# Old values issued behind their keys, and the sample states stored in two large pieces from ScalarE's queue

## Chip, cores and metric

The kernel runs on one core of a Trainium2 chip. The metric is the device time of one execution in microseconds, the median of several runs. Five engines run side by side and meet at semaphores: TensorE (PE), VectorE (DVE), ScalarE (ACT), GpSimd (POOL) and SyncE (SP). SyncE computes nothing here; its queue issues nearly all transfers.

## What is computed

One inference step of a two-layer decoder trunk in float32, for a prompt of 256 tokens and for 8 sampled sequences of 8 new tokens each. A layer is, cut to what matters:

```
h = RMSNorm(x); p = h @ w_in, split among three token mixers
A: dilated sliding-window attention, 8 heads of 64; the sampled tokens read a cache of 2048 old keys and values
B: RWKV-7 recurrence, 8 heads, state S (64 x 64 per head), which is also an output (new_wkv_*)
C: window attention, 16 query heads on 2 kv heads, old window of 128
x = x + concat(A, B, C) @ w_out
x = x + SwiGLU(RMSNorm(x))
```

The new keys, values, shift rows and states of both layers are outputs too.

## The kernel before

The weights stream through two raw buffers; ScalarE and VectorE split each block in a high and a low part, and TensorE multiplies with both. Between the projections `w_in` and `w_out` of a layer stand `rwkv(l)` and `attention(l)`, written out by hand in each engine's program. The change is in the queue around these two.

**Attention of the sampled tokens.** The 8 sequences are taken in pairs, q = 0 to 3. For a pair the old keys lie in `cK[0]` and `cK[1]`, the old values in `cV[0]` and `cV[1]`, each in three quads (4, 4 and 2 key tiles). For a pair:

- SyncE loads them with `cache(b, which, quad)` (L463 to L482): two loads of 512 KB for quads 0 and 1, one for quad 2, and a small one of 64 KB for the window cache (`ckc`, `cvc`). A sequence's keys are five large loads and one small, 2.6 MB, and its values the same.
- VectorE turns each quad of keys in place as it lands (`turn`, L1374), four transposes of the full size and two of half the size to a pair, waiting for each quad's own semaphore.
- TensorE computes the scores in `keys(q)`, with pieces of the prompt's attention placed between: `prompt_scores(a)`, and near its end `turned_probs(carry)`, which needs what ScalarE's `scale(carry)` wrote. Its last score product posts `sc`. Then come `probabilities(q)` and `values(q)`, which posts `pvq` once for each quad of values it is done with.
- ScalarE runs, for each pair, `exp(carry)`, `scale(carry)`, `exp(a)`, `turned_probs(carry)`, `scale(a)` and so on, and `exps(q)` for the samples. Here carry and a are the prompt's head pairs; for q = 0 they are 2 and 3. Ahead of `exps(0)` it waits for `snk`, which counts one small load and three stores of new keys.

The last pair (q = 3) has its values in `cK[0]` and in `cX`, the latter lying where the states are held until they are stored.

**SyncE's order in attention.** Keys of sequences 1 and 0; the small load `snk` (L492); a wait for `kvc`, which ScalarE posts when all nine blocks of new rows lie in `tk` (L837); three stores of new keys (L496, L497); values of sequences 0 and 1; seven stores of new values and window rows. Then for q = 1, 2, 3 `next_keys(q)`, which waits for `sc`, and `next_values(q)`, which waits for `pvq` quad by quad. Between the keys and the values of q = 1 stands `states_out()`. Before the load into `cX` at q = 2 SyncE waits until the states have left. Behind the last pair come the loads of `w_out`.

**The states.** ScalarE copies the states from PSUM to `Sout` (128 partitions: two head halves of 64; sequence, head, column) and `SoutP` for the prompt, and posts `Soc` (L849). This is done before attention starts. `states_out()` (L509 to L515) stores them with one transfer for each sequence and head half, 16 of 64 KB, and two for the prompt.

Of the kernel before, what the change touches and what calls it, by code (L numbers as in the profile page):

```python
# [39 lines left out]
DEPTH = 2  # L40
SEQ = 256
NB = 8
# [4 lines left out]
HD = 64  # L47
# [127 lines left out]
def build(nc, I, O, at):  # L175
    ctx = ExitStack()
    with ctx:
# [7 lines left out]
        def place(name, shape, offset, dt=F32):  # L185
            return nc.alloc_sbuf_tensor_at(name, shape, dt, offset=offset)
# [66 lines left out]
        Sout = place("Sout", [P, NB, 4, HD], RX + 10240)  # L253
        SoutP = place("SoutP", [P, 4, HD], RX)
# [44 lines left out]
        sem = {n: ctx.enter_context(nc.semaphore("s_" + n)) for n in names}  # L299
# [64 lines left out]
        def _(sp):  # L364
# [76 lines left out]
            for l in range(DEPTH):  # L441
# [21 lines left out]
                def cache(b, which, quad):  # L463

                    last = which == "V" and b // 2 == LASTQ
                    s = sem[f"cK{quad}{b % 2}" if last or which == "K" else f"cV{quad}"]
                    dst, small = (cK, ckc) if which == "K" or last else (cV, cvc)
                    ahead = last and b % 2 == 1
                    if ahead:
                        s = sem["cX"]  # L470
                    rows = I["cache_a_" + which.lower()][l, b].rearrange("r h d -> r (h d)")
                    old = rows[0:1536].rearrange("(j g r) c -> j g r c", j=3, r=16)
                    new = rows[1536:2048].rearrange("(p r) c -> p r c", p=P)
                    for j in range(2 * quad, min(2 * quad + 2, 5)):
                        to = (cX if ahead else dst[b % 2])[:, 2 * j:2 * j + 2, :]
                        if j < 3:
                            src = old[j, :, 0:8, :].rearrange("g (r i) c -> g r (i c)", i=2)
                            sp.dma_start(to.rearrange("p i c -> p (i c)"), src).then_inc(s, 16)  # L478
                        else:
                            sp.dma_start(to, new[:, 2 * j - 6:2 * j - 4, :]).then_inc(s, 16)  # L480
                    if quad == (2 if which == "K" or last else 1) and not ahead:
                        sp.dma_start(small[b % 2][:], I["cache_c_" + which.lower()][l, b].rearrange("r h d -> r (h d)")).then_inc(s, 16)  # L482
# [6 lines left out]
                cache(1, "K", 2)  # L489
                for quad in range(3):  # L490
                    cache(0, "K", quad)
                sp.dma_start(snk[:], I["c_sink"][l].rearrange("k g -> (k g)").unsqueeze(1).unsqueeze(2).broadcast_to([16, TS, 1])).then_inc(sem["snk"], 16)  # L492
                sp.wait_ge(sem["kvc"], 9 * (l + 1))
                for q in range(2):
                    rows = slice(q * P, (q + 1) * P)
                    sp.dma_start(O["new_a_k_prompt"][l, 0, rows].rearrange("t h d -> t (h d)"), tk[0][:, q, :]).then_inc(sem["snk"], 16)  # L496
                sp.dma_start(O["new_a_k_sample"][l].rearrange("b t h d -> (b t) (h d)"), tk[0][0:NS, 2, :]).then_inc(sem["snk"], 16)  # L497
                for quad in range(3):
                    cache(0, "V", quad)
                    cache(1, "V", quad)  # L500
                for q in range(2):
                    rows = slice(q * P, (q + 1) * P)
                    sp.dma_start(O["new_a_v_prompt"][l, 0, rows].rearrange("t h d -> t (h d)"), tk[1][:, q, :]).then_inc(sem["out"], 16)
# [1 line left out]
                sp.dma_start(O["new_c_v_prompt"][l, 0].rearrange("t h d -> t (h d)"), tk[2][:, 1, P:2 * P]).then_inc(sem["out"], 16)  # L505
                for name, src in (("new_a_v_sample", tk[1][0:NS, 2, :]), ("new_c_k_sample", tk[2][0:NS, 2, 0:P]), ("new_c_v_sample", tk[2][0:NS, 2, P:2 * P])):
                    sp.dma_start(O[name][l].rearrange("b t h d -> (b t) (h d)"), src).then_inc(sem["out"], 16)

                def states_out():  # L509
                    for h2 in range(2):  # L510
                        for b in range(NB):
                            sp.dma_start(O["new_wkv_sample"][l, b].rearrange("(f h) i j -> h i f j", h=2)[h2],  # L512
                                         Sout[h2 * HD:(h2 + 1) * HD, b]).then_inc(sem["souts"], 16)
                        sp.dma_start(O["new_wkv_prompt"][l, 0].rearrange("(f h) i j -> h i f j", h=2)[h2],
                                     SoutP[h2 * HD:(h2 + 1) * HD]).then_inc(sem["souts"], 16)  # L515

                def next_keys(q):
                    sp.wait_ge(sem["sc"], 4 * l + q)
                    for b2 in range(2):
                        for quad in range(3):  # L520
                            cache(2 * q + b2, "K", quad)

                def next_values(q):
                    if q == LASTQ:
                        sp.wait_ge(sem["sc"], 4 * l + q + 1)
                    for quad in range(3):
                        if q < LASTQ:
                            sp.wait_ge(sem["pvq"], 3 * (4 * l + q - 1) + quad + 1)
                        cache(2 * q, "V", quad)
                        if q < LASTQ:  # L530
                            cache(2 * q + 1, "V", quad)
                        elif quad == 2:
                            sp.dma_start(ckc[1][:], I["cache_c_v"][l, NB - 1].rearrange("r h d -> r (h d)")).then_inc(sem["cK21"], 16)
                for q in range(1, NB // 2):
                    next_keys(q)
                    if q == 1:
                        states_out()
                    if q == 2:
                        sp.wait_ge(sem["souts"], 16 * 18 * (l + 1))
                        for quad in range(3):  # L540
                            cache(NB - 1, "V", quad)
                    next_values(q)
# [16 lines left out]
            sp.wait_ge(sem["ends"], 80)  # L559
            sp.wait_ge(sem["out"], 16 * 9 * DEPTH)  # L560
            sp.wait_ge(sem["snk"], 64 * DEPTH)
            sp.wait_ge(sem["souts"], 16 * 18 * DEPTH)


        @block.gpsimd
# [62 lines left out]
        def _(act):  # L628
            want = Tally()

            def take(name, by=1):
                act.wait_ge(sem[name], want(sem[name], by))
# [151 lines left out]
            for l in range(DEPTH):  # L784
# [79 lines left out]
                def window_keys():  # L864
                    take("ktp")
                    act.activation(kcT[:].rearrange("p b k -> p (b k)"), PS[:, 7, 0:2 * P], ACT.Copy).then_inc(sem["ktc"], 1)
# [74 lines left out]
                turned_probs(1)  # L941
                output(1)
                window_keys()
                for q in range(NB // 2):
                    carry, a, b, c = partners(q)
                    exp(carry)
                    scale(carry)
                    exp(a)
                    turned_probs(carry)
                    scale(a)  # L950
                    output(carry)
                    turned_probs(a)
                    if q == 0:
                        act.wait_ge(sem["snk"], 64 * (l + 1))
                    exps(q)
                    output(a)
                    turned_sample(q)
                    if q < LASTQ:
                        query_rows(q + 1)
                        if b:  # L960
                            exp(b)
                            scale(b)
                            turned_probs(b)
                        window_keys()
                        if b:
                            output(b)
# [1178 lines left out]
```

## Time and profile before

| | |
|---|---|
| median of 3 runs | 3316.92 us (3314.89 to 3319.36) |
| the profiled execution's own time | 3315.85 us |
| its span, from the first instruction to the last | 3314.0 us |
| mean granted TensorE clock | 0.973 of full speed |
| TensorE busy | 3167.2 us, 96% |
| moved by DMA | 501.29 MB, 151 GB/s over the span |

Times in rows are microseconds from the span's start. A line such as L1374 is a line of the kernel. Where a row ends in brackets, the number in them is the idle time ahead of it and the arrow says what ended it. A DMA share of 1.00 means that all 16 DMA engines of the core were busy; values a little above 1 come from how packets are timed.

### The profile page before, as it was taken

The numbers are of one execution on the slowest core, as the hardware profiler recorded it, in microseconds if no ns is written. First come the engines' busy times: TensorE is split into PE (matmuls) and PEld (weight loads), VectorE is DVE, ScalarE is ACT, GpSimd is POOL, SyncE is SP. The second block draws the span as 40 slices with busy tenths as digits, with TensorE's granted clock in tenths as the row PEclk, the third lists the DMA queues.
The fourth block names the chain that finished last, engine by engine and source line by source line (L and its number), as shares of the span: only waits on it lengthen the run. The fifth ranks groups of instructions, "written<-read, shape, count | busy, mean of one in ns | idle before, by whom it ended". The sixth has DMA issues, their size and how long they took to land.

```text
span 3314.0 us, 62786 instructions
## 1 busy us (share of the span) xinstructions
PE 3167.2 (96%) x26351; PEld 3014.4 (91%) x26351; DVE 1756.7 (53%) x2112; ACT 1148.8 (35%) x1537; POOL 74.6 (2%) x157
## 2 busy tenths in 40 slices
PE   8999878899999999999999988789999999999998
PEld 7999755799999999999999987459999999999998
DVE  5555567455554454454545664765555545545544
ACT  3332264442332232322434313644323322323234
POOL 1000010000000000000000000100000000000000
PEclk9999888999999999999999998989999999999999
DMA  7553049765554554555565610787655545555454
GB/s 212 162 132 68 2 182 341 176 144 152 152 152 138 154 152 139 161 146 141 156 185 139 140 27 3 256 311 171 152 145 147 152 137 162 142 152 155 136 148 128
DMA packets 849061, 501.29 MB, mean 151 GB/s; under 512 B 96640, under 2 KB 823184, under 8 KB 848464
## 3 DMA queue, kind: packets, MB, share of 16 engines
q1 hardware_dynamic: 848492, 499.02, 53.7%
q8 instruction: 115, 1.88, 0.2%
q14 instruction: 34, 0.28, 0.0%
q10 hardware_dynamic: 420, 0.10, 0.0%
HBM read 485.71 MB, written 13.37 MB: 151 GB/s over the span
## 4 chain that ended last, share of the span: by engine, by line
PE 87%; DVE 4%; SPq 4%; DMA 3%; ACT 2%; issue 1%; POOL 0%; ACTq 0%; DVEq 0%
PE PS L1520 85%; DMA cK<-in_cache_a_k 2%; SPq L478 1%; PE PS L1521 1%; SPq L512 1%; DMA raw<-in_w_out 1%; SPq L480 1%; DVE cK L1374 0%; DVE wl L1010 0%; ACT wh L639 0%; SPq L482 0%; DVE S0T L1324 0%; DVE rt L1128 0%; ACT psm L876 0%; POOL S0in L588 0%
## 5 line engine op out<-in xcount | busy, mean ns | idle before, releaser
L639 ACT ACTIVATE wh<-raw 128x2048 fp32r<-128x2048 f32 (+1 forms) x408 | 711.7, 1744 | 1241.7 <-PE PS L1520 1211.1
L1010 DVE TENSOR_TENSOR wl<-raw,wh 128x2048 fp32r<-128x2048 f32 (+1 forms) x408 | 848.6, 2080 | 409.9 <-ACT wh L639 409.2
L1520 PE MATMUL PS<-fh,wh 128*128 128x320 f32 x2816 | 870.6, 309 | 0.0
L1520 PE MATMUL PS<-fh,wl 128*128 128x320 f32 x2816 | 870.1, 309 | 0.0
L1520 PE MATMUL PS<-fl,wh 128*128 128x320 f32 x2816 | 870.1, 309 | 0.0
L1520 PEld LDWEIGHTS PS<-fl,wh 128*128 128x128 f32 x2816 | 528.5, 188 | 0.2
L1520 PEld LDWEIGHTS PS<-fh,wh 128*128 128x128 f32 x2816 | 528.5, 188 | 0.2
L1520 PEld LDWEIGHTS PS<-fh,wl 128*128 128x128 f32 x2816 | 528.5, 188 | 0.0
L1520 PE MATMUL PS<-hh,wh 128*128 128x320 f32 (+2 forms) x1696 | 521.4, 314 | 1.6 <-DVE wl L1010 1.6
L1520 PE MATMUL PS<-hh,wl 128*128 128x320 f32 (+2 forms) x1696 | 513.3, 308 | 0.0
L1520 PE MATMUL PS<-hl,wh 128*128 128x320 f32 x1664 | 510.2, 310 | 0.0
L1520 PE MATMUL PS<-ah,wh 128*128 128x320 f32 x1408 | 435.7, 309 | 0.2 <-DVE wl L1010 0.2
L1520 PE MATMUL PS<-ah,wl 128*128 128x320 f32 x1408 | 435.1, 309 | 0.0
L1520 PE MATMUL PS<-al,wh 128*128 128x320 f32 x1408 | 435.0, 309 | 0.0
L1520 PEld LDWEIGHTS PS<-hh,wh 128*128 128x128 f32 x1696 | 318.0, 191 | 5.3 <-issue 1.9
L1520 PEld LDWEIGHTS PS<-hh,wl 128*128 128x128 f32 x1696 | 315.2, 189 | 0.0
L1520 PEld LDWEIGHTS PS<-hl,wh 128*128 128x128 f32 x1664 | 312.0, 188 | 1.4
L1520 PEld LDWEIGHTS PS<-ah,wh 128*128 128x128 f32 x1408 | 264.3, 188 | 0.8 <-issue 0.5
L1520 PEld LDWEIGHTS PS<-al,wh 128*128 128x128 f32 x1408 | 264.3, 188 | 0.0
L1520 PEld LDWEIGHTS PS<-ah,wl 128*128 128x128 f32 x1408 | 264.3, 188 | 0.0
L668 ACT ACTIVATE ge<-gt 128x320 f32<-128x320 f32 x88 | 41.5, 472 | 488.2 <-DVE gt L1050 488.2
L1050 DVE TENSOR_TENSOR gt<-PS,rsb 128x320 f32<-128x320 f32 x88 | 43.3, 492 | 226.1 <-PE PS L1520 226.1
(329 smaller groups left out, 2513.0 us busy)
## 6 DMA issues: line engine op xcount, KB each, us to landing
raw<-in_w_gate SPq DMA_DIRECT2D x88, 1024.0 KB, 5.6
raw<-in_w_up SPq DMA_DIRECT2D x88, 1024.0 KB, 5.6
raw<-in_w_down SPq DMA_DIRECT2D x128, 704.0 KB, 4.8
raw<-in_w_in SPq DMA_DIRECT2D x56, 1024.0 KB, 5.6
cK<-in_cache_a_k SPq DMA_DIRECT2D x80, 512.0 KB, 9.0
cV<-in_cache_a_v SPq DMA_DIRECT2D x60, 512.0 KB, 9.1
raw<-in_w_in SPq DMA_DIRECT2D x32, 512.0 KB, 5.6
raw<-in_w_out SPq DMA_DIRECT2D x32, 512.0 KB, 4.7
```

Source lines behind the costliest of these rows:

```text
L478: sp.dma_start(to.rearrange("p i c -> p (i c)"), src).then_inc(s, 16)
L480: sp.dma_start(to, new[:, 2 * j - 6:2 * j - 4, :]).then_inc(s, 16)
L512: sp.dma_start(O["new_wkv_sample"][l, b].rearrange("(f h) i j -> h i f j", h=2)[h2], Sout[h2 * HD:(h2 + 1) * HD, b]).then_inc(sem["souts"] ...
L639: act.activation(wh[j][:, 0:kts], raw[j][:, 0:kts], ACT.Copy).then_inc(sem["wh"], 1)
L668: act.activation(ge[:], gt[:], ACT.Tanh, scale=0.5).then_inc(sem["gexp"], 1)
L1010: tt(wl[j][:, 0:kts], raw[j][:, 0:kts], wh[j][:, 0:kts].bitcast(F32), ALU.subtract).then_inc(sem["wl"], 1)
L1050: tt(gt[:], PS[:, 0, 0:TOK], rsb[:], ALU.mult).then_inc(sem["ev"], 1)
L1520: mm = lambda out, lhsT, rhs, start=True, stop=True: pe.matmul(out, lhsT, rhs, start=start, stop=stop, skip_group_check=True)
L1521: tr = lambda out, x: pe.transpose(out, x, con[0:x.shape[0], at["ident"][0]:at["ident"][0] + x.shape[0]])
```

## The change

First, the values of sequences 0 and 1 are issued right behind the keys, ahead of the load `snk`, the wait for `kvc` and the stores of new keys. Second, `states_out()` is gone from SyncE. ScalarE issues the states' stores ahead of its loop over the pairs: for each head half one store with the states of all eight sequences (512 KB, 64 partitions of 8 KB in the buffer, 32 runs of 256 B for each partition in memory) and one for the prompt. The counts that wait for these stores go from 18 to 4 a layer.

```diff
                 for quad in range(3):
                     cache(0, "K", quad)
+                for quad in range(3):
+                    cache(0, "V", quad)
+                    cache(1, "V", quad)
                 sp.dma_start(snk[:], ...)
                 sp.wait_ge(sem["kvc"], 9 * (l + 1))
                 ...
-                for quad in range(3):
-                    cache(0, "V", quad)
-                    cache(1, "V", quad)
                 ...
-                def states_out():
-                    for h2 in range(2):
-                        for b in range(NB):
-                            sp.dma_start(O["new_wkv_sample"][l, b].rearrange("(f h) i j -> h i f j", h=2)[h2],
-                                         Sout[h2 * HD:(h2 + 1) * HD, b]).then_inc(sem["souts"], 16)
-                        sp.dma_start(O["new_wkv_prompt"][l, 0].rearrange("(f h) i j -> h i f j", h=2)[h2],
-                                     SoutP[h2 * HD:(h2 + 1) * HD]).then_inc(sem["souts"], 16)
                 ...
                 for q in range(1, NB // 2):
                     next_keys(q)
-                    if q == 1:
-                        states_out()
                     if q == 2:
-                        sp.wait_ge(sem["souts"], 16 * 18 * (l + 1))
+                        sp.wait_ge(sem["souts"], 16 * 4 * (l + 1))
...
                 output(1)
                 window_keys()
+                act.wait_ge(sem["Soc"], 9 * (l + 1))
+                for h2 in range(2):
+                    rows_h = slice(h2 * HD, (h2 + 1) * HD)
+                    act.dma_start(O["new_wkv_sample"][l].rearrange("b h i j -> (b h) i j").rearrange("(r h) i j -> h i r j", h=2)[h2],
+                                  Sout[rows_h].rearrange("p b f j -> p (b f) j")).then_inc(sem["souts"], 16)
+                    act.dma_start(O["new_wkv_prompt"][l, 0].rearrange("(f h) i j -> h i f j", h=2)[h2], SoutP[rows_h]).then_inc(sem["souts"], 16)
                 for q in range(NB // 2):
                     carry, a, b, c = partners(q)
                     exp(carry)
```

The query columns of `w_in` are loaded, far from the change, by two transfers for a block, each of 128 partitions by 16 runs of 256 B (L379); the prediction comes back to them.

## Rows read from the trace of the kernel before

**Rows 1.** The page's part 1: busy us (share of the span) xinstructions.

```profile
PE 3167.2 (96%) x26351; PEld 3014.4 (91%) x26351; DVE 1756.7 (53%) x2112; ACT 1148.8 (35%) x1537; POOL 74.6 (2%) x157
```

**Rows 2.** Chain that ended last, 450 to 615 us: shares, then start, us, what.

```profile
by line: PE PS L1520 22.6%; DMA cK<-in_cache_a_k 15.2%; SPq L478 11.6%; SPq L512 8.9%; DMA raw<-in_w_out 6.0%; issue 4.5%; SPq L480 4.5%; DVE cK L1374 4.2%; PE PS L1521 3.0%; SPq L482 2.5%; ACT psm L876 2.2%; ACT tk L837 1.9%; SPq L386 1.6%
...
527.15 14.34 DMA cK<-in_cache_a_k
```

**Rows 3.** SyncE's queue in order of time, layer 0: start, us, issues.

```profile
459.73 0.57 SPq L492 DMA_DIRECT2D snk<-in_c_sink  x1
471.04 0.82 SPq L496 DMA_DIRECT2D out_new_a_k_prompt<-tk  x2
...
472.52 3.24 SPq L478 DMA_DIRECT2D cV<-in_cache_a_v  x5
...
487.29 2.99 SPq L478 DMA_DIRECT2D cK<-in_cache_a_k  x3
...
495.45 10.09 SPq L512 DMA_DIRECT2D out_new_wkv_sample<-Sout  x8
...
512.17 3.54 SPq L478 DMA_DIRECT2D cV<-in_cache_a_v  x5
...
519.61 1.88 SPq L478 DMA_DIRECT2D cK<-in_cache_a_k  x3
```

**Rows 4.** Windows of 4.25 us: each engine's busy time, clock, DMA share, GB/s.

```profile
465.50:469.75 4.25, 3.61 (x21) 2.43 (x22) 4.21 (x4) 2.36 (x6) 0.00 (x0) 0.63 0.35 125
...
508.00:512.25 4.25, 3.35 (x84) 2.06 (x98) 3.04 (x7) 1.07 (x5) 0.00 (x0) 0.50 0.47 97
...
529.25:533.50 4.25, 4.25 (x72) 3.35 (x74) 3.39 (x4) 2.70 (x10) 0.00 (x0) 0.74 1.03 411
```

**Rows 5.** Waits over the whole span: us in total, times, longest.

```profile
DVE cK L1374 <- DMA cK<-in_cache_a_k: 13.2, 24, 3.2
```

**Rows 6.** VectorE in order of time: first turn of a pair's keys.

```profile
532.07 2.31 DVE L1374 STREAM_TRANSPOSE cK<-cK 128x2048 f32<-128x2048 f32 x1 [0.83 <-DMA cK<-in_cache_a_k]
...
565.25 2.31 DVE L1374 STREAM_TRANSPOSE cK<-cK 128x2048 f32<-128x2048 f32 x1 [1.34 <-DMA cK<-in_cache_a_k]
...
2127.05 2.31 DVE L1374 STREAM_TRANSPOSE cK<-cK 128x2048 f32<-128x2048 f32 x1 [2.03 <-DMA cK<-in_cache_a_k]
...
2166.22 2.31 DVE L1374 STREAM_TRANSPOSE cK<-cK 128x2048 f32<-128x2048 f32 x1 [3.25 <-DMA cK<-in_cache_a_k]
...
2199.20 2.31 DVE L1374 STREAM_TRANSPOSE cK<-cK 128x2048 f32<-128x2048 f32 x1 [0.54 <-DMA cK<-in_cache_a_k]
```

**Rows 7.** SyncE's queue, layer 1: the third pair's keys.

```profile
2155.04 1.83 SPq L478 DMA_DIRECT2D cK<-in_cache_a_k  x3
```

**Rows 8.** ScalarE in order of time, layer 0 and layer 1.

```profile
476.35 1.49 ACT L888 ACTIVATE psm<-psm,sums 128x128 f32<-128x128 f32 x4 [0.31 <-DVE sums L1365]
...
2107.97 1.49 ACT L888 ACTIVATE psm<-psm,sums 128x128 f32<-128x128 f32 x4 [0.31 <-DVE sums L1365]
2113.18 0.40 ACT L876 ACTIVATE psm<-psm,nm 128x128 f32<-128x128 f32 x1 [3.72 <-DVE nm L1358]
...
2121.03 1.41 ACT L903 ACTIVATE smA<-smA,snm 128x1344 f32<-128x1344 f32 x1
```

**Rows 9.** TensorE in order of time inside keys(0), both layers.

```profile
483.25 1.09 PE L1520 MATMUL PS<-cK,qd 32*32 32x320 f32 x31 [2.19 <-issue]
484.27 1.54 PE L1521 MATMUL PS<-con,psm 128*128 128x128 f32 x6
...
2113.35 0.55 PE L1521 MATMUL PS<-con,psm 128*128 128x128 f32 x3
2115.80 0.49 PE L1521 MATMUL PS<-con,psm 128*128 128x128 f32 x3 [1.90 <-issue]
```

**Rows 10.** State stores' issue durations (ns min/median/max); two loads of 2048 runs.

```profile
L512 SPq DMA_DIRECT2D out_new_wkv_sample<-Sout x32: 616/638/2389, 495.4 to 2144.1; - x32
...
207.65 2.02 SPq L379 DMA_DIRECT2D raw<-in_w_in  x2
```

More of the change, by code:

```diff
@@ L561, in _ @@
             sp.wait_ge(sem["snk"], 64 * DEPTH)
-            sp.wait_ge(sem["souts"], 16 * 18 * DEPTH)
+            sp.wait_ge(sem["souts"], 16 * 4 * DEPTH)
         @block.gpsimd
```

## Prediction

> **What bounds the kernel now.** I read the page's table of busy times first. TensorE is busy 96% of a span of 3314.0 us [rows 1], so over most of the kernel no transfer can buy anything. That is an average over stages, so next comes the chain of work that ended last, asked only for the stretch of layer 0's attention that the change touches, 450 to 615 us. There TensorE's busiest line holds 22.6%, a transfer of old keys 15.2%, and lines of SyncE's queue 11.6% (L478, cache loads), 8.9% (L512, the state stores) and more [rows 2]. This stage is set by loads and by the queue that issues them.
>
> The queue's timeline shows how [rows 3]. SyncE has issued the first pair's keys by 459.73. It then stands at the wait for `kvc` until 471.04 and issues the first pair's values only at 472.52. Keys(1), the second pair's, go out at 487.29, when TensorE has finished with the first. Then come 18 state stores, from 495.45 until 512.17, and only behind them the second pair's values, 512.17 to 519.57, and the third pair's keys, from 519.61.
>
> The table by windows shows what this leaves of the DMA engines [rows 4]. They are empty two thirds of the time at 465.5 to 469.75 (share 0.35), when SyncE waits, and half the time at 508.00 to 512.25 (share 0.47, 97 GB/s), when only state stores are there. Where big loads are queued they run full, 411 GB/s. I use 405 GB/s. A pair's keys, ten loads of 512 KB and two small ones, are 5.2 MB and take 12.9 us; its values take as long.
>
> Who waits for the keys is VectorE, whose transposes (L1374) feed the scores. Its 24 waits for them sum to 13.2 us [rows 5]. It turns a pair's keys in about 11.9 us when nothing is late: four transposes of 2.31 us [rows 6], two of half the size, and small operations between. The instruction before each turn is its own, so each such wait lies on the loop that sets the stage: keys landed, turned, scores, `sc`, next keys issued. Gaps at the first turn of a pair are 0.83 and 1.34 us in layer 0, and 2.03, 3.25 and 0.54 us in layer 1 [rows 6].
>
> **The change, part by part.**
>
> *Values(0) and (1) ahead of the wait.* These are 15 cache loads and the two small ones inside them, all on SyncE. They are moved ahead of one sink load and three key stores; nothing is added. Issue starts at 459.73. The keys' remaining transfer comes first in the same queue, so I take it as undisturbed. Keys are done by about 466.7 and values by 466.7 + 12.9 = 479.6 instead of about 487. The stores of new rows (1.47 MB, 3.7 us) follow, to 483.3. The wait for `kvc` is then reached near its end, perhaps 2 us late, and the rest is issued before 487.29. ScalarE waits for the sink load and the three key stores only ahead of `exps(0)`, where its next work starts at 2121.03 in layer 1 [rows 8]; they should land by about 2114 to 2120. Cost nothing; if that cover fails, about 1 us.
>
> *State stores off SyncE.* 18 issues vanish, 16.7 us of its time (495.45 to 512.17), a median of 0.64 us each with stalls on top [rows 10]. SyncE can then issue the second pair's values behind `pvq`, whose quads TensorE releases before 504, in place of 512.17. The next keys go at `sc`.
>
> What is late next? For each later pair I ask whether its keys can land before VectorE wants them; VectorE's new start is that of its row, less the gap and less what was gained before (532.07 - 0.83 - 0.8 = 530.4; 565.25 - 1.34 - 2.6 = 561.3). Layer 0: keys(1) from 487.3 land by 502, and VectorE starts at 495.1 and needs its last quad at about 505. Values(1) are through by 515. Keys(2) go at about 518.6 and land by 533; VectorE starts at 530.4 and needs the last at 541. Then come the odd last value load and values(2), to about 552. Keys(3) go at 554.7 and land by 569; VectorE is ready at 561.3 and needs the last at 572. Layer 1 is tighter for keys(1), since the stores on ScalarE's queue still run at 2117. They land by 2136, with about 1 us to spare. Keys(2) there were issued at 2155.04 by a late SyncE [rows 7] and can now go at 2148.4, since keys(1) start 2.6 us sooner. So VectorE bounds each loop and its key waits go. The sum is 24 waits, 13.2 us, less 1.0 us kept for pieces that will not close: **-12.2 us**. No other work hides it: the loop runs from each turn through the scores to the next pair's keys, on to `w_out`, and the stage after it waits for all.
>
> *Four issues on ScalarE.* They stand in front of exp(2), so exp(2), scale(2), exp(3), and behind them TensorE's turned_probs(2) in the middle of keys(0), queue up behind them. The added wait for `Soc` is for ScalarE's own earlier copies, done long before. The slack is read off the timelines. In layer 0 scale(2) ends at 476.35 + 1.49 = 477.84, and TensorE takes its result at 484.27 [rows 8, 9]: 6.4 us. In layer 1 it ends at 2109.46 and exp(3) starts at 2113.18, after 3.72 us idle; TensorE turns at 2113.35, slack 3.9 us, with a hole of 1.90 us of its own before 2115.80.
>
> The price of an issue is not shown for this shape on this queue. From below: four issues at the 0.62 us of SyncE's state stores [rows 10] are 2.5 us, and cost nothing. The nearest row by pieces is the query columns of `w_in`. There two loads of 128 x 16 runs of 256 B, the same 2048 runs as one new store, were issued back to back in 2.02 us [rows 10]. With two small ones at 0.62 that makes 3.3 us, inside both slacks. From above: the last issue may have to wait until the first store and its small one have drained. Drained beside loads: 97 GB/s at share 0.47 is 206 GB/s of full engines, so a layer's 1.18 MB of states is 5.7 us of engine time and half of it 2.9 us. If SyncE's backlog (474.3 to 483.3, 9.0 us) goes through alongside, the stall is 11.9 us, costing 11.9 - 6.4 = 5.5 us in layer 0 and 11.9 - 3.9 = 8.0 us in layer 1, **0 to +13.5 us**. I take 0, by the nearest row.
>
> Full engines are seen here behind one queue only [rows 4]. A rule of the Trainium skill speaks against the change at this point. The Trainium skill, "DMA: Bandwidth & Descriptors", section "Queues, rings and completion order", says that each DMA engine alternates between the queue rows that have work, a packet at a time. By it the 256 B runs and the 4 KB runs of the values take turns, so the stores drain slowly while the backlog lasts, and the sum would lean to the upper end, near 0 instead of -12.2; that is the mechanism of rivals A and B. No row here has two busy queues, so the trace neither agrees nor disagrees.
>
> **Sum.** The profiled execution took 3315.85 us, 1.07 below the median of the three runs, 3316.92. 3315.85 - 12.2 = 3303.7; against the median 3304.7. I say **3305 us**.
>
> **The rivals.**
>
> *A: ScalarE stalls part of the way (chance 0.22).* Two queues share the engines and the second store is held 5 to 11 us. For it: SyncE's own state-store issues stretch to 2.39 us at the worst, behind queued loads [rows 10]. Against it: the 2.02 us pair. Cost 0 to 11.7 us over both layers, say 5: about 3310, between 3306 and 3316.
>
> *B: ScalarE stands until both stores are gone (0.07), the one that ends slower.* The place is the issue of the last store. If it is held until all of SyncE's backlog and all 5.7 us of states are through, that is 14.7 us from 474.3 to 489: 8.3 us over the slack in layer 0 and 10.8 in layer 1, 19.1 against a gain of 12.2, so about 3324. It decides above a hold of 11.3 us per layer, where (11.3 - 6.4) + (11.3 - 3.9) = 12.3 eats the gain. Against it: it takes a queue that accepts nothing while 2048 runs are pending, and [rows 10] had a second such load accepted within 2 us of the first.
>
> *C: the waits go but the time only moves (0.16).* The bytes are the same, and later pairs are loaded at the full rate either way (411 GB/s at 529 to 533 [rows 4]). If keys(2) and (3) stay at the engines' pace behind values, or TensorE's holes of 2 us "for nothing that the profile shows" (2.19 us inside keys(0) [rows 9]) fall in other places, only 4 to 8 us are gained: 3308 to 3313. For it: the third pair's last keys took 14.34 us to land [rows 2]. Against it: that was behind values issued late, and the idle stretches of [rows 4] are what the change fills.
>
> *Forecast (0.55):* all key waits gone and ScalarE inside its slack, own range 3299 to 3309; its low end is the whole 13.2 us and 4 us for TensorE, which ran at a granted clock of 0.50 after such a wait [rows 4].
>
> **Numbers.** Within 0.2% is about what a measurement of this kernel can tell from no change: 6.6 us, so faster means below 3310.3. Faster: 0.54 of the forecast, 0.09 of A, 0.07 of C, 0.70. Slower: B and its edge, 0.08. Same: 0.22. The range runs from the forecast's low end to the far end of A, 3299 to 3316.
>
> **What would show it.** Right: values(0) issued from 460; nothing idle at 465 to 470 but the engines full; keys(1) landed before each turn; VectorE's key waits near 1 us in total instead of 13.2; third pair's keys at 518 to 519; four issues on ScalarE taking under 4 us in each layer. Wrong: an issue on ScalarE longer than 3 us with exp(2) behind it, keys(0) ending later than 488 in layer 0, or transposes that still wait for keys.

## The result and the profile after

The changed kernel takes 3323.63 us, the median of 12 runs (3320.81 to 3328.14). The kernel before, measured again beside it, takes 3318.21 (12 runs, 3313.59 to 3322.15). The ratio is 1.002, 95% interval 1.0011 to 1.0029: slower by 0.2%, 5.4 us by the two medians and some 6.6 us by the ratio, where 12 us of gain were forecast. The time lies above the range. It is the one that rival B named, 3324. The profiled execution took 3323.82 us with a span of 3322.0 us, 8.0 us longer than before.

The page's part 1 after, beside [rows 1]:

```profile
PE 3160.4 (95%) x26351; PEld 3011.2 (91%) x26351; DVE 1755.5 (53%) x2112; ACT 1148.5 (35%) x1537; POOL 74.6 (2%) x157
```

No engine has more to do; the time is waiting. The waits over the whole span (us in total, times, longest) say whose:

```profile
ACT psm L866 <- issue: 27.5, 2, 14.5
...
DVE cK L1370 <- DMA cK<-in_cache_a_k: 2.3, 6, 0.6
```

The lower line is the one forecast. VectorE's waits for the keys are down from 13.2 us in 24 waits [rows 5] to 2.3 us in 6. The upper line is new. Before exp(2), ScalarE stands "for issue", twice and 27.5 us in all, that is once in each layer. What it does in that time is on its own timeline, layer 0 first and then layer 1 (start, us, what; ACTq is ScalarE's queue of issues):

```profile
474.81 0.72 ACTq L937 DMA_DIRECT2D out_new_wkv_sample<-Sout  x1
475.56 7.50 ACTq L939 DMA_DIRECT2D out_new_wkv_prompt<-SoutP  x1
483.09 2.30 ACTq L937 DMA_DIRECT2D out_new_wkv_sample<-Sout  x1
485.42 4.24 ACTq L939 DMA_DIRECT2D out_new_wkv_prompt<-SoutP  x1
489.71 0.40 ACT L866 ACTIVATE psm<-psm,nm 128x128 f32<-128x128 f32 x1 [14.53 <-issue]
...
2114.09 7.35 ACTq L939 DMA_DIRECT2D out_new_wkv_prompt<-SoutP  x1
...
2126.77 0.40 ACT L866 ACTIVATE psm<-psm,nm 128x128 f32<-128x128 f32 x1 [12.98 <-issue]
```

The first large store is accepted in 0.72 us. The small one behind it takes 7.50 us to issue, the second large one 2.30 and its small one 4.24. The four take 14.8 us (474.81 to 489.66) where 3.3 was assumed. TensorE's timeline shows what queues behind them, the turned_probs(2) of [rows 9]:

```profile
493.43 1.54 PE L1517 MATMUL PS<-con,psm 128*128 128x128 f32 x6 [9.28 <-ACT psm L878]
```

It began at 484.27 before; now TensorE idles 9.28 us for ScalarE's scale(2). The table by windows (length, each engine's busy time, granted clock, DMA share, GB/s) shows both sides of the change, beside [rows 4]:

```profile
465.50:469.75 4.25, 2.69 (x17) 1.65 (x18) 4.21 (x5) 3.28 (x9) 0.00 (x0) 0.74 1.02 392
482.50:486.75 4.25, 0.83 (x31) 0.24 (x31) 0.00 (x0) 0.00 (x0) 0.00 (x0) 0.75 1.08 343
486.75:491.00 4.25, 0.00 (x0) 0.00 (x0) 0.00 (x0) 1.29 (x7) 0.00 (x0) 0.50 0.85 188
495.25:499.50 4.25, 4.25 (x48) 2.55 (x16) 2.45 (x7) 2.61 (x8) 1.22 (x8) 0.50 0.35 88
499.50:503.75 4.25, 2.78 (x14) 1.88 (x14) 2.36 (x4) 2.36 (x3) 0.71 (x5) 0.50 0.99 364
503.75:508.00 4.25, 4.25 (x24) 3.23 (x22) 2.06 (x4) 2.45 (x10) 0.00 (x0) 0.50 1.02 406
508.00:512.25 4.25, 4.25 (x83) 2.67 (x84) 4.25 (x2) 3.31 (x19) 0.00 (x0) 0.94 0.98 388
```

At 465.5 to 469.75 the DMA engines are full (1.02, 392 GB/s; the share was 0.35 before), as intended. From 482.5 to 491 three compute engines do next to nothing. After this idle time the granted clock is 0.50, the 1.2 GHz level, up to 508, though TensorE is busy again (4.25 of 4.25 us in two of these windows); it works through the rest of keys(0) and the work behind it at half the clock. Low windows are nothing new in themselves: before, the clock was 0.50 at 508.00 to 512.25 [rows 4].

SyncE's queue shows where the time goes on, beside [rows 3] and [rows 7]:

```profile
460.84 3.12 SPq L478 DMA_DIRECT2D cV<-in_cache_a_v  x5
...
496.45 1.90 SPq L478 DMA_DIRECT2D cK<-in_cache_a_k  x3
...
533.25 1.83 SPq L478 DMA_DIRECT2D cK<-in_cache_a_k  x3
...
2133.50 1.89 SPq L478 DMA_DIRECT2D cK<-in_cache_a_k  x3
...
2166.85 2.50 SPq L478 DMA_DIRECT2D cK<-in_cache_a_k  x3
```

Keys(1) of layer 0 leave at 496.45 instead of 487.29, 9.2 us late, of which 0.9 were there on entry to the stage. The third pair's leave at 533.25 instead of 519.61, 13.6 us late: this loop takes 36.8 us (496.45 to 533.25) where it took 32.3 before, so it loses instead of gaining. The clock is down for its first 11.5 us; the section on the reasons comes back to that. Only behind that do the absent key waits pay, and the first load of `w_out` is issued at 600.87 against 592.93, 7.9 us late. Layer 1 starts 6.5 us late and loses 9.0 more up to keys(1) (2133.50 against 2117.97). Then it gains 7.0 back (`w_out` 8.5 us late). In layer 0 only 1.3 us come back behind keys(1).

### The profile page after: what moved, and what is told of

It is laid out like the page before. It is cut to its first block, busy times and chain, and to the rows that moved or that the text cites. A ratio compares the mean times of both kernels' runs of the same rounds, so it can differ in the third digit from the quotient of the medians.

```text
span 3322.0 us, 62758 instructions
## 1 busy us (share of the span) xinstructions
PE 3160.4 (95%) x26351; PEld 3011.2 (91%) x26351; DVE 1755.5 (53%) x2112; ACT 1148.5 (35%) x1537; POOL 74.6 (2%) x157
## 4 chain that ended last, share of the span: by engine, by line
PE 88%; DVE 5%; ACT 2%; DMA 2%; issue 1%; ACTq 1%; SPq 1%; POOL 0%; DVEq 0%
PE PS L1516 86%; PE PS L1517 2%; DVE cK L1370 1%; ACTq L939 1%; DMA cK<-in_cache_a_k 1%; DMA raw<-in_w_out 1%; ACT psm L866 0%; DVE wl L1006 0%; ACT wh L629 0%; SPq L478 0%; DVE S0T L1320 0%; DVE rt L1124 0%; ACT psm L878 0%; ACT ppt L883 0%; DMA raw<-in_w_in 0%
```

## The experiments

Ratios are to the kernel before, run beside on the same chip, with 95% intervals. Its medians in the three groups were 3316.4 (23 runs; e1 to e4), 3317.76 (16; e5 to e8) and 3317.82 (35; e9 to e12). Microseconds faster or slower are worked out from the ratio. "Hold" is the wait of exp(2) for issue.

### The two parts alone

**e1_values_first**: the first part of the change alone; the 18 stores stay on SyncE where they were.

```diff
                 for quad in range(3):
                     cache(0, "K", quad)
+                for quad in range(3):
+                    cache(0, "V", quad)
+                    cache(1, "V", quad)
                 sp.dma_start(snk[:], ...)
```

> Only the first part of the change: values(0) issued right behind the keys, the 18 state stores stay on SyncE's queue behind the second pair's keys. Theory 1 (the change lost by the hold of ScalarE alone, its loads' part was right): no hold on ScalarE, exp(2) starts as before at about 474; VectorE's waits for keys fall from 13.2 us to 3 to 7 us, since the state stores still delay the second pair's values and, in layer 1, the third pair's keys; 5 to 10 us faster than before, ratio 0.997 to 0.9985. Theory 2 (early values bring nothing, the time only moves): ratio 0.999 to 1.001.

Measured: 3312.73 us (12 runs), ratio 0.9987 (0.9978 to 0.9996). The waits for keys do not fall:

```profile
DVE cK L1374 <- DMA cK<-in_cache_a_k: 14.5, 14, 4.7
```

There are fewer of them and they are longer. SyncE still issues the states' stores from 490.70 to 508.11, ahead of the second pair's values and the third pair's keys (516.58).

**e2_big_on_act**: the second part alone; as changed, but the first pair's values back at their old place behind the wait for `kvc`.

```diff
-                for quad in range(3):
-                    cache(0, "V", quad)
-                    cache(1, "V", quad)
                 sp.dma_start(snk[:], ...)
                 ...
+                for quad in range(3):
+                    cache(0, "V", quad)
+                    cache(1, "V", quad)
```

> Only the second part of the change: the four state stores on ScalarE's queue, values(0) at their old place behind the three key stores. Theory 1 (two queues share the engines, and ScalarE stands until its stores have drained beside SyncE's loads): values(0) are issued from 472 and stand beside the stores, so ScalarE is held 12 to 16 us in each layer as in the changed kernel; keys(0) ends about 8 to 10 us late, SyncE gives back less than that; 3 to 15 us slower than before, ratio 1.001 to 1.0045. Theory 2 (the hold came from the backlog that the early values had built up by 474): hold under 8 us and the time within 0.1% of before or better.

Measured: 3333.12 us (6 runs), ratio 1.0055 (1.0043 to 1.0067); the profiled execution, 3323.84 us, was the quickest of the six. The hold grows to 20.3 us a layer:

```profile
ACT psm L866 <- issue: 40.3, 2, 20.3
...
DVE cK L1370 <- DMA cK<-in_cache_a_k: 2.0, 5, 0.8
```

So the early values do not cause the hold. In both kernels SyncE's transfers run beside the stores. And with the stores on ScalarE the key waits are nearly gone, whether the values are early (2.3 us) or not (2.0). Beside such stores early values are worth more than alone: 1.0055 without them, 1.002 with them.

### What holds ScalarE

**e3_small_on_act**: as changed, but with 18 small stores on ScalarE's queue.

```diff
-                    act.dma_start(... all eight sequences ..., Sout[rows_h] ...)
+                    for b in range(NB):
+                        act.dma_start(O["new_wkv_sample"][l, b].rearrange("(f h) i j -> h i f j", h=2)[h2], Sout[rows_h, b])
```

> The changed kernel with the states in 18 small stores on ScalarE's queue in place of four. Theory 1 (the hold is set by how fast 4608 runs of 256 B drain beside the loads, whatever the number of stores): first about eight issues at 0.6 us each, later ones stretched, 12 to 16 us in total, time within 0.15% of the changed kernel. Theory 2 (a large store has an issue price of its own): 18 x 0.64 = 11.5 us evenly, exp(2) 3 us earlier than in the changed kernel.

Measured: 3330.07 us (5 runs), ratio 1.0043 (1.003 to 1.0056). ScalarE's queue:

```profile
472.05 7.32 ACTq L938 DMA_DIRECT2D out_new_wkv_sample<-Sout  x8
479.39 1.73 ACTq L940 DMA_DIRECT2D out_new_wkv_prompt<-SoutP  x1
481.15 7.59 ACTq L938 DMA_DIRECT2D out_new_wkv_sample<-Sout  x8
```

The hold is 17.0 us with 18 stores against 14.5 with four (17.7 against 13.0 in layer 1). Fourteen more issues make 2.5 and 4.7 us of it; the same bytes and pieces go with the rest. Here too the profiled execution, 3324.38 us, was the quickest.

**e6_no_loads_beside**: as changed, but SyncE waits until the states have left before it issues the first pair's values, so nothing else is in the DMA engines.

```diff
-                for quad in range(3):
-                    cache(0, "V", quad)
-                    cache(1, "V", quad)
...
+                sp.wait_ge(sem["souts"], 16 * 4 * (l + 1))
+                for quad in range(3):
+                    cache(0, "V", quad)
+                    cache(1, "V", quad)
```

> The four state stores on ScalarE's queue with values(0) behind them: SyncE waits for the stores' end before it issues values(0), so hardly any load stands beside the stores. A look at the hold of ScalarE only. Theory 1 (a queue stands once about 2048 short runs are pending, and its runs drain slowly because another queue's 4 KB runs take turns with them): alone the 4352 runs drain in 5 to 6 us, so the hold is 4 to 6 us instead of 13 to 20. Theory 2 (these issues have a price of their own on ScalarE): 13 us or more still.

Measured in one run: 3328.2 us; its time is that of values issued late (at 482.78; key waits 22.7 us) and is not compared. The hold is what it was made for:

```profile
474.00 0.72 ACTq L938 DMA_DIRECT2D out_new_wkv_sample<-Sout  x1
474.76 1.54 ACTq L940 DMA_DIRECT2D out_new_wkv_prompt<-SoutP  x1
476.33 1.44 ACTq L938 DMA_DIRECT2D out_new_wkv_sample<-Sout  x1
477.80 1.67 ACTq L940 DMA_DIRECT2D out_new_wkv_prompt<-SoutP  x1
479.51 0.40 ACT L867 ACTIVATE psm<-psm,nm 128x128 f32<-128x128 f32 x1 [5.13 <-issue]
```

The same four stores hold ScalarE 5.1 us in layer 0 and 6.6 in layer 1 instead of 14.5 and 13.0. The loads beside them make the rest, 9.4 and 6.4 us. The DMA view says how (queue: packets, MB, share of 16 engines; q1 is SyncE's, q10 ScalarE's). First the changed kernel, 476 to 478 us and then 480 to 482 us:

```profile
q1 hardware_dynamic: 240, 0.80, 101.0%
...
q1 hardware_dynamic: 341, 0.66, 85.8%
q10 hardware_dynamic: 342, 0.09, 19.4%
```

And this one, 474 to 480 us:

```profile
DMA packets 3518, 0.91 MB, mean 151 GB/s; under 512 B 3517, under 2 KB 3517, under 8 KB 3517
q10 hardware_dynamic: 3517, 0.89, 67.9%
```

Two things happen beside SyncE's backlog. The first store, issued from 474.81, has moved nothing by 478; its first records come between 478.5 and 479, some 4 us after the issue began. With no loads beside them they come within 1.5 us (issued from 474.00, first records between 475 and 475.5). Then the two queues take turns record by record: 342 to 341 here, and 1255 to 1236 from 480 to 486. SyncE's records there carry 1.5 KB on average and ScalarE's 256 B, so ScalarE's queue gets 0.32 MB in those 6 us, 53 GB/s. Alone it moves 0.40 MB in 2 us (476 to 478 in this run), 200 GB/s. The first store has landed 4.5 us after its issue there and 13.0 us after it here, and the issues behind it wait.

**e7_small_first**: as changed, but both small stores ahead of both large ones.

```diff
                 for h2 in range(2):
                     rows_h = slice(h2 * HD, (h2 + 1) * HD)
+                    act.dma_start(... prompt ..., SoutP[rows_h])
+                for h2 in range(2):
+                    rows_h = slice(h2 * HD, (h2 + 1) * HD)
                     act.dma_start(... sample ..., Sout[rows_h] ...)
-                    act.dma_start(... prompt ..., SoutP[rows_h])
```

> The changed kernel with the two small prompt stores ahead of the two large ones. A look at single issues only. Theory 1 (whichever store comes behind 2048 pending runs is held): two small ones 0.6 us each, the first large one under 2 us, the last large one 7 to 12 us. Theory 2 (the prompt store's shape is what is slow): the two small ones take 4 to 8 us each though nothing is pending.

Measured in one run: 3312.84 us.

```profile
474.59 1.39 ACTq L937 DMA_DIRECT2D out_new_wkv_prompt<-SoutP  x2
476.01 9.67 ACTq L940 DMA_DIRECT2D out_new_wkv_sample<-Sout  x2
485.73 0.40 ACT L866 ACTIVATE psm<-psm,nm 128x128 f32<-128x128 f32 x1 [10.76 <-issue]
```

Now the small ones issue in 0.7 us each. Of the two large ones the first takes 0.64 us and the second 9.0. The small store is dear only behind a large one that has not left, and so is a second large one. With nothing behind the second large store, the hold is 10.8 and 9.7 us instead of 14.5 and 13.0.

### The hold by itself

**e8_states_on_pool**: early values, and the 18 small stores on GpSimd's queue, behind its copies for the third pair. ScalarE issues nothing.

```diff
-                    if q == 1:
-                        states_out()
...
+                    if q == 2:
+                        pool.wait_ge(sem["Soc"], 9 * (l + 1))
+                        for h2 in range(2):
+                            for b in range(NB):
+                                pool.dma_start(O["new_wkv_sample"][l, b]..., Sout[rows_h, b]).then_inc(sem["souts"], 16)
+                            pool.dma_start(O["new_wkv_prompt"][l, 0]..., SoutP[rows_h]).then_inc(sem["souts"], 16)
```

> Values first, and the 18 small state stores on GpSimd's queue behind its copies for the third pair, at about 492 in layer 0. GpSimd has slack of tens of us there. Theory 1 (the loss is that an engine on the path stands at the issues; on an engine with slack the whole gain is kept): no hold on ScalarE or SyncE, VectorE's key waits 2 to 5 us, 9 to 13 us faster than before, ratio 0.996 to 0.9973. Theory 2 (the stores beside the loads cost by themselves, through keys that land late): key waits above 8 us and ratio above 0.998.

Measured: 3307.14 us (6 runs), ratio 0.9972 (0.9959 to 0.9984), 9.3 us faster than before. Key waits are 6.6 us in 10, and SyncE is late with `cX`: it waits from 527.92 to 532.38 for the last of the stores, which GpSimd issues three at a time with gaps of 3.7 to 6.9 us.

**e9_pool_and_idle_hold**: e8, and on ScalarE, where the four issues stood, ten copies into a buffer that is free there. No transfer is added.

```diff
+                for n in range(10):
+                    act.activation(smA[:], con[:, 0:1344], ACT.Copy).then_inc(sem["hold"], 1)
+                    act.wait_ge(sem["hold"], 10 * l + n + 1)
                 for q in range(NB // 2):
```

> The kernel with the states on GpSimd's queue and, where the changed kernel has its four issues, ten copies on ScalarE of a table into a free buffer (about 14.5 us, no transfer at all). It adds work that computes nothing. Theory 1 (ScalarE's standing alone is the loss): TensorE idles about 9 to 10 us in keys(0) of each layer, about 16 to 22 us slower than the same kernel without the hold, so ratio to before 1.001 to 1.004, like the changed kernel. Theory 2 (what is lost in the changed kernel is lost by stores and loads sharing the engines): under 12 us slower than without the hold, ratio below 1.0005.

Measured: 3322.88 us (11 runs), ratio 1.0019 (1.0011 to 1.0028), the changed kernel's 1.002 again. ScalarE's timeline, TensorE's, and two windows:

```profile
473.06 13.51 ACT L943 ACTIVATE smA<-con 128x1344 f32<-128x1344 f32 x10
```

```profile
490.32 1.54 PE L1522 MATMUL PS<-con,psm 128*128 128x128 f32 x6 [8.05 <-ACT psm L886]
```

```profile
486.00:490.00 4.00, 0.00 (x0) 0.00 (x0) 1.37 (x3) 3.65 (x13) 0.00 (x0) 0.50 0.01 2
490.00:494.00 4.00, 3.68 (x43) 2.33 (x43) 1.54 (x5) 3.45 (x13) 0.00 (x0) 0.50 0.00 0
```

ScalarE is held 13.5 us by plain work, TensorE idles 8.05 us at the same place and the granted clock goes to 0.50, with the DMA engines empty. Against e8 that costs 1.0019 - 0.9972 = 0.0047, 15.6 us, give or take 5 by the two intervals. The hold alone explains the loss; contention for the transfers themselves is not needed.

**e10_pool_and_short_hold**: e9 with two copies in place of ten (2.67 us in layer 0), to test the slack.

```diff
-                for n in range(10):
+                for n in range(2):
```

> As the kernel before, with two copies in place of ten (about 3 us). Tests the slack of 3.9 and 6.4 us that the prediction read off the timelines. Theory 1 (that slack is real): no different from the kernel without a hold, ratio 0.9965 to 0.998. Theory 2 (ScalarE has no slack here): 5 to 6 us slower than without the hold, ratio 0.9985 to 0.9995.

Measured: 3310.03 us (11 runs), ratio 0.998 (0.997 to 0.999). By time that is 2.7 us slower than e8, but the two intervals leave room for anything from none to 8, so the time alone doesn't settle it. TensorE's waits for ScalarE's scaled products do, here in e8, e9 and e10:

```profile
PE PS L1519 <- ACT psm L886: 1.9, 4, 0.6
...
PE PS L1522 <- ACT psm L886: 18.4, 6, 8.4
...
PE PS L1522 <- ACT psm L886: 1.9, 4, 0.6
```

Two copies leave them as they are without a hold, ten add 16.5 us. The short hold does not reach TensorE, so the slack is real.

### The stores elsewhere

**e4_values_first_big_on_sp**: early values; the four stores in their new shape, on SyncE at the old place.

```diff
                     for h2 in range(2):
-                        for b in range(NB):
-                            sp.dma_start(O["new_wkv_sample"][l, b]..., Sout[h2 * HD:(h2 + 1) * HD, b])
+                        sp.dma_start(... all eight sequences ..., Sout[h2 * HD:(h2 + 1) * HD] ...)
                         sp.dma_start(... prompt ...)
```

> Values first, and the states in four large stores on SyncE's queue at the old place, behind the second pair's keys. Theory 1 (a queue stands once about 2048 short runs are pending, so large stores save SyncE nothing): the four issues take 8 to 16 us together and the time is within 0.1% of the same kernel with 18 small stores. Theory 2 (large stores are cheap on SyncE and only ScalarE's queue is slow): four issues under 4 us, second pair's values issued from about 500, 3 to 5 us faster than the kernel with 18 small ones.

Measured: 3307.3 us (12 runs), ratio 0.9976 (0.9967 to 0.9984). SyncE's queue shows the same hold on another queue:

```profile
491.61 0.65 SPq L511 DMA_DIRECT2D out_new_wkv_sample<-Sout  x1
492.31 9.38 SPq L513 DMA_DIRECT2D out_new_wkv_prompt<-SoutP  x1
501.73 1.42 SPq L511 DMA_DIRECT2D out_new_wkv_sample<-Sout  x1
503.19 1.56 SPq L513 DMA_DIRECT2D out_new_wkv_prompt<-SoutP  x1
```

The four take 13.1 us against 17.4 for the eighteen of e1, behind keys(1) that are still in the queue. But SyncE computes nothing, so all that waits is the next load, which is issued at 504.80. Key waits are 5.7 us in 11. The issues take what theory 1 said, but the kernel is 0.11% quicker than e1, nearer to theory 2; the intervals of the two overlap.

**e5_states_behind_values1**: early values; the 18 small stores on SyncE, moved behind the second pair's values.

```diff
                     next_keys(q)
-                    if q == 1:
-                        states_out()
...
                     next_values(q)
+                    if q == 1:
+                        states_out()
```

> Values first, and the 18 small state stores on SyncE's queue behind the second pair's values, where SyncE would wait for the second pair's scores. Theory 1 (what is left in the kernel with only the values first is the state stores standing ahead of the second pair's values and the third pair's keys): SyncE reaches the stores at about 505 and is done at about 519 to 522, so the third pair's keys leave at most 3 us late; VectorE's key waits 3 to 6 us; 8 to 12 us faster than before, ratio 0.9965 to 0.9975. Theory 2 (the place of the stores does not matter): like the kernel with only the values first, 0.9987.

Measured: 3309.69 us (11 runs), ratio 0.9979 (0.997 to 0.9988), key waits 10.9 us in 16. The stores, 503.05 to 521.74, now delay the third pair's keys to 521.78.

**e12_big_behind_values1**: e5 with the four large stores.

```diff
                     next_values(q)
+                    if q == 1:
+                        states_out()      # four stores, as in e4
```

> Values first, four large state stores on SyncE's queue behind the second pair's values. Theory 1 (a held queue costs nothing where its engine would wait anyway, and the hold of four large stores, about 13 us, is shorter than 18 small ones' 18.7 us): SyncE is free by about 516, the third pair's keys leave as soon as sc allows, VectorE's key waits 2 to 6 us, 10 to 13 us faster than before, ratio 0.996 to 0.9972. Theory 2 (only the place counts): like the 18 small stores in this place, 0.9979.

Measured: 3307.84 us (11 runs), ratio 0.9974 (0.9965 to 0.9982), key waits 4.5 us in 8. The four take from 504.74 to 519.17, the one behind the first large store 10.73 us of it. By time e4, e5 and e12 can't be told apart, so on SyncE neither the place nor the shape of the stores is shown to matter.

**e11_pool_last_values_later**: e8, with the wait for the states and the load into `cX` moved behind the third pair's values, so that SyncE isn't held in front of them.

```diff
                 for q in range(1, NB // 2):
                     next_keys(q)
+                    next_values(q)
                     if q == 2:
                         sp.wait_ge(sem["souts"], 16 * 18 * (l + 1))
                         ...
-                    next_values(q)
```

> States on GpSimd's queue, and the load into cX with its wait for the states moved behind the third pair's values. In the kernel with the states on GpSimd's queue SyncE stood 4.5 us at that wait in layer 0. Theory 1 (that wait delays values and with them the last pair's keys): 1 to 3 us faster than that kernel, ratio 0.996 to 0.9975. Theory 2 (the later load only changes places with others): the same within 1 us.

Measured: 3305.48 us (12 runs), ratio 0.9971 (0.996 to 0.9981), key waits 6.2 us in 12. It is the quickest kernel of the study, 9.6 us faster than before and some 16 faster than the changed one, though not told apart from e8, e4 or e12 by its interval.

## Why the prediction was wrong

**What bounds the stage: right.** VectorE's waits for the keys were on the loop, and SyncE's lateness made them. With the stores off SyncE's queue they fell from 13.2 us to 2.3.

**Values ahead of the wait: right, but small by itself.** Values(0) were issued from 460.84 and the DMA engines were full at 465 to 470, as foretold. Alone this gains 0.13% (e1), some 4 us: the stores on SyncE keep the rest.

**State stores off SyncE, -12.2 us: nearly right in size.** The waits that went are 10.9 us (what stays open there is below). With no issue on ScalarE the whole gain is 9.3 us (e8) or 9.6 (e11), with 6.6 and 6.2 us of key waits left; -12.2 lies inside both intervals. The stores need not leave SyncE for that: early values and four large stores on SyncE gain 8.0 us (e4) and 8.6 (e12). The mark "third pair's keys at 518 to 519" was missed, at 533.25, for the next reason.

**Four issues on ScalarE, 0: this step failed.** They cost 14.5 us of ScalarE in layer 0 and 13.0 in layer 1. The nearest row, two loads of 2048 runs in 2.02 us [rows 10], had the right number of pieces and the wrong surroundings. With no loads beside them the four stores hold ScalarE 5.1 and 6.6 us (e6). Beside SyncE's backlog their queue starts 4 us late and then gets 53 GB/s instead of 200, and everything behind the first large store is held. The upper bound, 11.9 us, was too low as well: it let the last issue go when only half the states had drained. At 490, just after the last issue went at 489.66, 4255 of the 4608 state records had moved.

**The slacks, 6.4 and 3.9 us: right.** By them the hold costs 14.5 - 6.4 = 8.1 us in layer 0 and 13.0 - 3.9 = 9.1 in layer 1, 17.2 together. From the stage's first key load to the first load of keys(1) the changed kernel takes 8.3 and 9.0 us longer than the kernel before. In e7 the holds of 10.8 and 9.7 us give 4.4 and 5.8 by the slacks, and the stretch is 4.5 and 5.8 longer. With longer holds the rule gives a little too much: e2, 13.9 and 16.2 against 12.8 and 14.7. The sum then comes near: 3315.85 - 10.9 + 17.2 = 3322.2 us against 3323.82 of the profiled execution. That it comes so near is in part luck: single executions differ by as much as 6 us at the start of this stage, ahead of everything that was changed (440.43 in e2, 446.70 before), and a slow return of the clock, below, is not in the sum.

**Rival A** had the mechanism, two queues that share the engines, but not the size. **Rival B** had both, at a chance of 0.07: a hold of 14.7 us, until all of SyncE's backlog and all of the states are through, and 3324 us. Its hold is met to 0.2 us in layer 0; in layer 1 it was 13.0. That the time is met to 0.4 us is luck in part: both of its terms were somewhat too large, 19.1 us of cost (17.2 by the measured holds) against 12.2 of gain (10.9). It was put at 0.07 on the ground that [rows 10] show a second load accepted at once while 2048 runs are pending. In e6 too the issues behind the first large store are accepted in 1.4 to 1.7 us (0.6 to 2.8 in layer 1), where the runs leave quickly. At [rows 10] no other transfer was under way either (DMA share 0.00 at 206 to 208 us). That row told of a queue that drains, not of one that is starved. The point from which B decides, a hold of 11.3 us a layer, held up as far as one run can show it: e7, with 10.8 and 9.7 us, came out at 3312.84, below all 16 runs of the kernel before in its group (3314.05 the lowest). **Rival C** is what e1 shows, for the first part alone.

**Two queues at once.** Where both queues have records to move, they take turns one by one: 342 to 341 at 480 to 482 us, and 438 to 441 at 2118 to 2120 in layer 1. The rule of the Trainium skill that the prediction names, "DMA: Bandwidth & Descriptors", "Queues, rings and completion order", that each DMA engine alternates between the queue rows with work, is borne out. By the prediction's own reading of it the sum would have leaned to its upper end, the side on which the result fell. What the rows add is the 4 us that pass before the first store's records take part in these turns. The same page of the Trainium skill, "Issuing engines are not separate DMA queues", says that issuing from several engines only saves the time that the sequencer needs to start a transfer, "which is usually small relative to the DMA itself". Here that time was not small: the four issues took 14.8 us, and the change moved them from an engine that computes nothing to one that TensorE waits for.

**What stays open.** How many runs a queue takes before it holds the next issue was not measured; the runs show only that one store of 2048 behind another waits beside loads. Nor is it shown why the first record of such a store comes 4 us late beside loads. Of the 10.9 us of key waits that went in the changed kernel, a part may be owed to the hold itself, which gives loads more time to land. Its 2.3 us that are left are fewer than the 6.6 of e8, but there GpSimd's slow stores delay SyncE too. Layer 0 should have gained about 4.6 us behind the hold (its share of the forecast -12.2) and gained 1.3. The traces point at the clock for the difference. After a hold and an idle stretch of the same kind the level of 2.4 GHz came back sooner in other kernels, for example in e2, where TensorE had idled 15.3 us at this place. Its keys(1) and keys(2), and the window that was at 0.50 in the changed kernel:

```profile
493.84 1.88 SPq L478 DMA_DIRECT2D cK<-in_cache_a_k  x3
...
526.55 1.83 SPq L478 DMA_DIRECT2D cK<-in_cache_a_k  x3
```

```profile
495.25:499.50 4.25, 2.77 (x26) 1.77 (x25) 3.61 (x6) 2.09 (x4) 1.93 (x12) 0.98 0.90 297
```

Its loop takes 32.7 us, and so does that of e3 (32.9), e7 (32.9) and e9 (32.8), against 36.8 in the changed kernel, so some 4 us of its profiled execution go with the late return of the clock. In its own layer 1 the level was back by the window 2136 to 2139 (0.89) and the loop took 33.4. Why it came back late in layer 0, and in how many of the twelve executions it did, is open. What the idle time costs by itself and what the low clock right behind it costs is not separated either, since e9 has both.

## What to carry to other kernels

Before transfers are moved to a computing engine's queue, ask what that engine's next instruction is, who waits for it, and how fast the queue will drain at that moment: price the issue as the drain of what stands before it, beside all that the other queues hold, and not by an issue in a quiet stretch. A stall on an engine that computes nothing can be cheaper than a shorter one on the path: with early values, eighteen stores that took 18.7 us of SyncE in layer 0 (e5) left the kernel 0.21% faster than before, and four that took 14.8 us of ScalarE there made it 0.2% slower. When the price of one step is unknown and its upper bound turns the sign, that bound deserves more than a few per cent.

## What the runs showed of the hardware

- A store of 64 partitions by 32 runs of 256 B is accepted in 0.64 to 0.72 us on a queue where no other large store is pending (on ScalarE's, and 0.65 on SyncE's behind loads in e4; 1.02 and 1.61 behind loads in e12). The first one behind it takes 1.5 us (2.8 in layer 1) with no loads beside it (e6) and 7.4 to 11.1 us beside loads of 512 KB, whether it is small (256 runs) or large, on ScalarE's queue or SyncE's.
- Two queues with work share the engines record by record, not by bytes: 342 records of 256 B to 341 of the other queue, 0.09 MB to 0.66 MB, in 2 us of full engines; the same in layer 1 (438 to 441) and in e2 (273 to 269 at 474 to 476). Pieces of 256 B alone move at about 200 GB/s (0.40 MB in 2 us, e6).
- The first record of such a store on ScalarE's queue came some 4 us after its issue began where SyncE's queue was full, and within 1.5 us where it was empty (e6).
- GpSimd issued such stores of 64 KB at 0.62 us each, but only two or three at a time, with gaps of 3.7 to 6.9 us beside loads in layer 0 (1.8 to 6.7 in layer 1). Eighteen took some 37 us (489.56 to 527.2 in e8).
- After 9.3 us of idle TensorE the granted clock was 0.50 until 508, some 15 us after work had started again at 493.4. After 15.3 us of it in e2, with work again from 490.8, it was 0.98 in the window 495.25 to 499.50. The length of the idle stretch alone doesn't tell when the clock comes back.
